# Latents' norm inside the projection, and index scores, queries and keys as one program

## The reference, cut to what matters

```python
mod = cond @ w_ada[l] + b_ada[l]
sh1, sc1, gt1, sh2, sc2, gt2 = [m[:, None, :] for m in jnp.split(mod, 6, axis=-1)]
h = rms_norm(x, g_pre_mix[l]) * (1.0 + sc1) + sh1
proj = h @ w_in[l]
(c_q, c_kv, k_rope, q_d, k_d, v_d, q_idx, k_idx, w_idx) = jnp.split(proj, split_at, axis=-1)
y_mla = mla_attention(c_q, c_kv, k_rope, positions, g_q_a[l], g_kv_a[l], w_q_b[l], w_kv_b[l])
y_dsa = dsa_attention(q_d, k_d, v_d, q_idx, k_idx, w_idx, positions)
mix = jnp.concatenate([y_mla, y_dsa], axis=-1) @ w_o[l]
x = x + gt1 * rms_norm(mix, g_post_mix[l])
h2 = rms_norm(x, g_pre_ffn[l]) * (1.0 + sc2) + sh2
ffn = moe_ffn(h2, w_router[l], b_router[l], w_mlp1[l], b_mlp1[l], w_mlp2[l], b_mlp2[l])
```

## Time and profile before

| | |
|---|---|
| Median of 3 runs | 3205.06 us (3203.02 to 3207.84) |
| The profiled execution | 3207.77 us |
| Its span in the profile | 3206.0 us, granted clock 0.919 on average |
| Busy: PE, DVE, ACT, POOL | 2899.5, 2155.3, 1628.3, 180.7 us |
| First mixer, up to the residual | about 515 us |

### The profile page before, as it was taken

One profiled execution on the slowest core, in us unless ns is written; L12 is line 12 of the kernel. 1 busy time (PEld: TensorE's weight loads), 2 busy tenths in 40 slices (PEclk: granted clock), 3 DMA queues, 4 the chain that ended last, 5 costly groups with the idle time before them and its releaser, 6 DMA issues. The chain is left out here.

```text
span 3206.0 us, 40971 instructions
## 1 busy us (share of the span) xinstructions
PE 2899.5 (90%) x13449; PEld 2295.6 (72%) x13449; DVE 2155.3 (67%) x3059; ACT 1628.3 (51%) x2117; POOL 180.7 (6%) x137
## 2 busy tenths in 40 slices
PE   7758895399999999999998698899999988899998
PEld 6636574278888888888887475578887765588887
DVE  5459635399999999999997764654444465554444
ACT  6323422378888888888886324433222324342222
POOL 2600200200000000000000300000000000000000
PEclk9865576699999999999999798999999999999999
DMA  7439512399999999999997521132332320233222
GB/s 267 144 113 353 212 54 112 132 355 386 389 391 376 390 390 386 381 391 389 381 384 294 190 69 38 53 99 92 99 99 92 112 59 27 67 105 98 93 85 92
DMA packets 292798, 660.39 MB, mean 206 GB/s; under 512 B 21850, under 2 KB 146538, under 8 KB 292676
## 3 DMA queue, kind: packets, MB, share of 16 engines
q1 hardware_dynamic: 275890, 603.45, 51.0%
q0 software_dynamic: 10816, 37.11, 3.1%
q10 hardware_dynamic: 5970, 18.21, 1.4%
HBM read 583.12 MB, written 75.58 MB: 205 GB/s over the span
## 5 line engine op out<-in xcount | busy, mean ns | idle before, releaser
L1530 DVE TENSOR_TENSOR weights_low<-pieces,weights_high 128x1024 fp32r<-128x1024 f32 x768 | 890.4, 1220 | 72.2 <-ACT weights_high L1523 63.0
L1523 ACT ACTIVATE weights_high<-pieces 128x1024 fp32r<-128x1024 f32 x768 | 804.9, 1062 | 201.3 <-PE banks L378 201.2
L376 PE MATMUL banks<-weights_high,xT_high 128*128 128x512 f32 x1024 | 403.1, 394 | 1.3 <-DVE weights_low L1530 1.3
L377 PE MATMUL banks<-weights_low,xT_high 128*128 128x512 f32 x1024 | 399.6, 390 | 0.0
L378 PE MATMUL banks<-weights_high,xT_low 128*128 128x512 f32 x1024 | 399.1, 390 | 0.0
L2145 ACT ACTIVATE weights_high<-pieces 128x1024 fp32r<-128x1024 f32 x192 | 200.8, 1053 | 322.6 <-DMA pieces<-in_w_up 248.9
L2149 DVE TENSOR_TENSOR weights_low<-pieces,weights_high 128x1024 fp32r<-128x1024 f32 x192 | 233.6, 1223 | 126.2 <-ACT weights_high L2145 124.9
L376 PE MATMUL banks<-hT_high,weights_high 128*128 128x512 f32 x704 | 284.3, 404 | 2.8 <-DVE hT_low L3171 2.8
L377 PE MATMUL banks<-hT_low,weights_high 128*128 128x512 f32 x704 | 276.3, 393 | 0.0
L378 PE MATMUL banks<-hT_high,weights_low 128*128 128x512 f32 x704 | 275.5, 391 | 0.0
L376 PEld LDWEIGHTS banks<-weights_high,xT_high 128*128 128x128 f32 x1024 | 192.8, 188 | 52.9 <-issue 13.5
(11 more groups left out here) (448 smaller groups left out, 4662.3 us busy)
## 6 DMA issues: line engine op xcount, KB each, us to landing
pieces<-in_w_mlp SPq DMA_DIRECT2D x768, 512.0 KB, 7.7
expert_out<-mask SPq DMA_DIRECT2D x32, 1536.0 KB, 15.0
pieces<-in_w_up SPq DMA_DIRECT2D x64, 512.0 KB, 3.9
pieces<-in_w_down SPq DMA_DIRECT2D x64, 512.0 KB, 3.3
pieces<-in_w_in SPq DMA_DIRECT2D x56, 512.0 KB, 4.8
pieces<-in_w_ada SPq DMA_DIRECT2D x48, 512.0 KB, 5.1
expert_out<-y ACTq DMA_DIRECT2D x32, 512.0 KB, 7.8
pieces<-in_w_out SPq DMA_DIRECT2D x16, 512.0 KB, 4.8
```

The costliest lines, as they stand in the source:

```text
L376: nc.tensor.matmul(out, a[0], b[0], start=start, stop=False)
L377: nc.tensor.matmul(out, a[0], b[1], start=False, stop=False)
L1523: self.core.nc.scalar.activation(self.hi[:, c % E_PARTS, :], self.raw[:, c % E_RAW, :], ACT.Copy).then_inc(self.high.sem, 1)
L1530: self.core.nc.vector.tensor_tensor(self.lo[:, c % E_PARTS, :], self.raw[:, c % E_RAW, :], self.hi[:, c % E_PARTS, :], ALU.subtract).then_ ...
```

## The change

The late jobs leave the projection and the opening: 20 run in the second attention (three in four units from the seventh) and 15 in the product with w_o, two behind each piece from the third on; the zero writes are now six and five there, one behind every third load. The ring places that held late pieces in the projection hold the latents' weights (`Latents`), which SP loads first in the projection. The squares, the root, the scalings and the transposes of the latents, and the rotation of the shared key, are done inside `projection_stage`, while the second and third column blocks run; it uses six banks and leaves two for the transposes. `index_stages` and the rest of `mla_stages` ahead of the attention become `middle_stage`, one block: for each tile PE makes queries, keys and values, then six index scores (two banks), then turns queries and keys (through the same two banks). ACT instead of DVE copies keys and values out. Relu buffers are four instead of two.

```diff
-LATE_FIRST, LATE_SECOND = 24, 11
+LATE_FIRST, LATE_SECOND = 20, 15
...
-def projection_stage(core, pieces, hT, xT, cols, widths, proj, late):
+def projection_stage(core, pieces, hT, xT, cols, widths, proj, latent, cos, sin, W):
...
-        @block.gpsimd
-        def _(pool):
-            late.add(pool, LATE_FIRST)
         @block.sync
         def _(sp):
+            latent.load(sp, W)
             for q in range(count * PIECES - pieces.places):
                 pieces.load_piece(sp, count * PIECES)
-            late.load(sp, LATE_FIRST)
...
-            for p in range(first + PIECES, first + count * PIECES):
+            for p in range(first + PIECES, first + 2 * PIECES):
                 pieces.split_high(act, p)
-                late.scale(act, LATE_FIRST // (2 * PIECES))
-            late.scale(act, LATE_FIRST - late.scaling)
+            for i in range(2 * T):
+                act.wait_ge(*taken(i % T + 1))
+                if i:
+                    act.wait_ge(*squares(i))
+                part = proj[:, i % T, OFF1[i // T]:OFF1[i // T + 1]]
+                nc.scalar.activation(core.junk[:, 0, 0:part.shape[1]], part, ACT.Square, accum_out=stats[:, 6 * T + i:6 * T + i + 1]).then_inc(squares.sem, 1)
+            pieces.split_high(act, first + 2 * PIECES)
+            act.wait_ge(*spread(1))
+            nc.scalar.activation(rt, ms, ACT.Sqrt).then_inc(root.sem, 1)
+            for c in range(3):
+                act.wait_ge(*lat_turned(c + 1))
+                nc.scalar.activation(latent.latT[:, c, :], core.psum[:, 6 + c % 2, :], ACT.Copy).then_inc(lat_taken.sem, 1)
+            for p in range(first + 2 * PIECES + 1, first + 3 * PIECES):
+                pieces.split_high(act, p)
...
-                    if k == 0 and i >= 8:
-                        pe.wait_ge(*taken(i - 7))
+                    if k == 0 and i >= 6:
+                        pe.wait_ge(*taken(i - 5))
...
+                    last = product_in_parts(nc, core.psum[:, i % 6, 0:width], tokens, w, k == 0, k == KD - 1)
+                    if n == 1 and k == KD - 1 and t == 2:
+                        for c in range(3):
+                            pe.wait_ge(*lat_ready(1))
+                            if c == 2:
+                                pe.wait_ge(*lat_taken(1))
+                            for s in range(T):
+                                last = nc.tensor.transpose(core.psum[:, 6 + c % 2, s * P:(s + 1) * P], proj[:, s, c * P:(c + 1) * P], core.ident[:])
+                            last.then_inc(lat_turned.sem, 1)
...
             for n in range(count):
                 for t in range(T):
                     i = n * T + t
-                    if n + 1 < count:
-                        pieces.split_low(dve, first + (n + 1) * PIECES + t)
+                    if n == 0:
+                        pieces.split_low(dve, first + PIECES + t)
+                    if n == 1 and t in (0, 3):
+                        pieces.split_low(dve, first + 2 * PIECES + t // 3)
+                    if n == 2 and t == 0:
+                        pieces.split_low(dve, first + 2 * PIECES + 2)
+                        pieces.split_low(dve, first + 2 * PIECES + 3)
                     dve.wait_ge(*(product(n * (T - 1) + t + 1) if t < T - 1 else pieces.used(first + (n + 1) * PIECES)))
-                    nc.vector.tensor_copy(proj[:, t, n * BANK:n * BANK + widths[n]], core.psum[:, i % 8, 0:widths[n]]).then_inc(taken.sem, 1)
+                    if n == 1 and t == 0:
+                        dve.wait_ge(*squares(2 * T))
...
+                    if n == 1 and t == 1:
+                        dve.wait_ge(*root(1))
+                        step(nc.vector.reciprocal(rstd, rt))
+                        dve.wait_ge(*latent.gains_full(32))
+                        for s in range(T):
+                            cq, ckv = proj[:, s, 0:Q_RANK], proj[:, s, OFF1[1]:OFF1[2]]
+                            nc.vector.scalar_tensor_tensor(out=cq, in0=cq, scalar=rstd[:, s:s + 1], in1=latent.gq, op0=ALU.mult, op1=ALU.mult)
+                            ins = nc.vector.scalar_tensor_tensor(out=ckv, in0=ckv, scalar=rstd[:, T + s:T + s + 1], in1=latent.gkv, op0=ALU.mult, op1=ALU.mult)
+                        ins.then_inc(lat_ready.sem, 1)
+                    if n == 2 and t == 0:
+                        for s in range(T):
+                            rotate(nc, step, latent.krot[:, s], proj[:, s, OFF1[2]:OFF1[3]].unsqueeze(1), cos[:, s, :], sin[:, s, :], latent.tmp, 1, ROPE // 2)
...
         with nc.Block() as block:
             @block.sync
             def _(sp):
-                pieces.load_ahead(sp, count * PIECES)
+                for i in range(LATE_SECOND):
+                    late.load(sp, 1)
+                    if i % 3 == 2:
+                        aside(sp, range(E - LATE_SECOND // 3 + i // 3, E - LATE_SECOND // 3 + i // 3 + 1))
+            @block.gpsimd
+            def _(pool):
+                late.add(pool, LATE_SECOND)
             @block.scalar
             def _(act):
                 for p in range(first, first + count * PIECES):
                     pieces.split_high(act, p)
+                    if p >= first + 2:
+                        late.scale(act, 2)
+                late.scale(act, LATE_SECOND)
...
-                    late.add(pool, LATE_SECOND)
+                    late.add(pool, LATE_FIRST)
...
-                    if late is not None and u >= H1 and u % 2:
-                        late.scale(act, 1)
+                    if late is not None and u >= 6 and u % 4 != 3:
+                        late.scale(act, min(1, LATE_FIRST - late.scaling))
...
                 pieces.load_ahead(sp, count * PIECES)
-                late.load(sp, late.places)
...
+    def __init__(self, core, ring):
+        flat = ring.rearrange("p a n -> p (a n)")
+        self.latT = flat[:, 0:3 * S].rearrange("p (c n) -> p c n", c=3)
+        self.wq = flat[:, 3 * S:3 * S + 2 * H1 * QK1].rearrange("p (c n) -> p c n", c=2)
+        self.wkv = flat[:, 3 * S + 2 * H1 * QK1:3 * S + 2 * H1 * QK1 + H1 * (NOPE + VDIM)]
+        spare = core.junk[:, 0, :]
+        self.tmp = spare[:, 256:256 + 4 * (ROPE // 2)].rearrange("p (a h n) -> p a h n", a=4, h=1)
+        self.gq, self.gkv = spare[:, 512:512 + Q_RANK], spare[:, 768:768 + KV_RANK]
+        self.krot = spare[:, 896:896 + T * ROPE].rearrange("p (t h n) -> p t h n", t=T, h=1)
...
+            def _(pe):
+                def turn_index():
+                    for c in range(2):
+                        for t in range(T):
+                            last = nc.tensor.transpose(core.psum[:, 4 + c, t * P:(t + 1) * P], proj[:, t, qio + c * P:qio + (c + 1) * P], core.ident[:])
+                        last.then_inc(idx_turned.sem, 1)
...
+                def make(t):
+                    tile = slice(t * P, (t + 1) * P)
+                    if t:
+                        pe.wait_ge(*rotated(t))
+                        pe.wait_ge(*k_rows(t))
+                    w = 4 * QK1
+                    for n in range(2):
+                        for c in range(2):
+                            last = nc.tensor.matmul(core.psum[:, n, 0:w], latT[:, c, tile], wq[:, c, n * w:(n + 1) * w], start=(c == 0), stop=(c == 1))
+                    last.then_inc(q_made.sem, 1)
+                    for n in range(2):
+                        last = nc.tensor.matmul(core.psum[:, 2 + n, :], latT[:, 2, tile], wkv[:, n * BANK:(n + 1) * BANK], start=True, stop=True)
+                    last.then_inc(kv_made.sem, 1)
+                def scores(i):
+                    t, h = tiles[i]
+                    if i >= 2:
+                        pe.wait_ge(*relu(i - 1))
+                    g = (h % 4) * IDX_D
+                    nc.tensor.matmul(core.psum[:, 6 + i % 2, 0:(t + 1) * P], qiT[g:g + IDX_D, h // 4, t * P:(t + 1) * P], kiT[g:g + IDX_D, 0:(t + 1) * P], start=True, stop=True).then_inc(score.sem, 1)
+                def turn(src, j):
+                    if j:
+                        pe.wait_ge(*taken(2 * j))
+                    for h in range(H1):
+                        last = nc.tensor.transpose(core.psum[0:QK1, 4 + h // 4, (h % 4) * P:(h % 4 + 1) * P], src[:, h, :], core.ident[:])
+                    last.then_inc(turned.sem, 1)
+                turn_index()
+                pe.wait_ge(*latent.weights_full(32))
+                make(0)
+                pe.wait_ge(*idx_taken_a(2))
+                pe.wait_ge(*idx_taken_d(1))
+                for t in range(T):
+                    if t:
+                        make(t)
+                    for i in range(6 * t, 6 * t + 6):
+                        scores(i)
+                    pe.wait_ge(*rotated(t + 1))
+                    turn(qk, 2 * t)
+                    pe.wait_ge(*k_rows(t + 1))
+                    pe.wait_ge(*k_rope(t + 1))
+                    turn(kk, 2 * t + 1)
+                def take_index(j, dst, bank):
+                    act.wait_ge(*idx_turned(j))
```

(110 more changed lines are left out.)

208 lines of the change are left out of this document (44 added, 164 removed).

## The result

The kernel after took 3173.05 us in the median (3168.78 to 3177.7), the kernel before beside it 3204.95 (3203.02 to 3207.84): a ratio of 0.990 (95% interval 0.9883 to 0.9917), 31.9 us faster. The forecast was 3170.3 with a range of 3153 to 3191. The profiled execution has a span of 3175.6 us against 3206.0, 30.4 less.

A forecast was written before the change was run, and what follows sets the result against it. Each stage had its own limit: the projection PE's waits behind late jobs, the first attention DVE, the second PE. Terms -15.7 - 24.6 + 1.5 + 4 = -34.8 took 3205.1 to 3170.3 us, range 3153 to 3191.

The forecast's parts named there:

- Term 1: Projection: late jobs leave it and the latents' norm hides under the product, only its transposes on the path; minus 15.7 us.
- Rival F: Projection: scaled latents ready many us behind PE's third tile, so it only trades its waits; total 3186 us, chance 4%.
- Term 2: Middle: one block of 61 us instead of 85.6, at a granted clock of 0.8; minus 24.6 us.
- Rival D: Middle: runs at full clock in 52 us; total 3161.3 us, chance 13%.
- Term 3: Second attention: nine more late scales on ACT and adds on POOL cost time in the first tiles; plus 1.5 us.
- Term 4: Product with w_o: ACT's late scales wait for loads and delay weight splits that PE needs; plus 4 us.
- B: Middle: runs at half clock in 84 us; total 3193.3 us, chance 10%.
- C: Late jobs hold PE again in their new places and all 15.7 us come back; total 3180.5 us, chance 15%.
- E: Second attention and product: each group of late loads and a zero write takes 17.4 us; total 3232 us, chance 3%.

The follow-up runs named there:

- the filled kernel: Kernel after with one added TensorE product per middle tile, placed in the wait before the keys are turned: middle 54.8 us, total 3162.52 us (one execution).
- both edits together: Kernel after with keys turned into banks 2 and 3 and the product's first four late loads issued in the second attention: 3155.59 us, ratio 0.9851 to before.
- the early transfers alone: Kernel after with the first four late loads of the product issued at the end of SyncE's list in the second attention: 3167.64 us, ratio 0.9893 to before.
- the kernel with the keys' banks: Kernel after with keys turned into banks 2 and 3, so PE does not wait for ACT's query copies: 3157.64 us, ratio 0.9852, middle 47.5 us.

## Why the prediction held, and where it did not

**Term 1, right.** -15.3 against -15.7: the last matmul ended at about 122.5 where 123.5 was forecast (the opening's 1.4 us are in that), the latents were ready 1.7 us ahead of PE's question for them, the margin of the forecast, both 1.5 us earlier, and the transposes cost the 1.9 us that I had put on the path (46.2 against 44.3 without the norm). The split of 1.22 us in the earlier trace rows, read as one alone, had an addition of POOL beside it (from 62.05, 5.41 us); the value held all the same, as the second block's pieces were split in 1.22 us with POOL gone. Rival F, that the projection trades its waits, is out.

**Term 2, right in its parts, off by the clock.** The waits are those that I named. I took a granted clock of 0.8 from the tiles of the earlier trace rows; it was 0.74. The formula of the forecast, 52 + 32 x (1/clock - 1) + 1, gives 64.2 us for 0.74, and 63.6 were measured; for 0.96 it gives 54.3, less the 5.0 of waits 49.3, and 47.5 were measured. The failed step is to take the clock as given. It moved with the pauses that the new order leaves. The earlier trace rows could have warned: transposes at half clock stood close behind the idle time of the rotation. I read this as a price of transposes, but the first eight of the earlier trace rows ran at full, 1.08 us, as did those of the keys in the filled kernel, 1.04. Nor does one pause set the pace of the next group: that 1.08 stands right behind 3.20 us of idle time.

Rival D, full clock in the middle, nearly came true once the pause of 1.26 us per tile was gone or filled: 0.96 and 0.91, at 47.5 and 54.8 us. The Trainium skill, "TensorE: Matmul & The Clock Gate", Part 1, describes a kernel in which short idle moments between groups of matmuls make the clock swing between its levels; the pair with and without filled waits agrees (0.91 against 0.74). The Trainium skill's rule in the same part, that sustained work brings the full clock, is again not borne out by the second attention, where PE was busy 88.6 of 88.6 us at 0.50.

**Term 3, right by number, wrong by reason.** +1.6 against +1.5, but the late jobs cost nothing: without them the stage took 113.5. What went is a part of the stretch at full clock near its start (0.67 against 0.85 over 9.8 us). The step that nine more scalings and additions push PE in the first tiles failed: PE's own time covers them. That the number fitted is luck. Why the identical set-up is granted the full clock for longer in some executions is open: both kernels with the old middle had it (111.9), and one in nine with the new. With PE kept busy ahead of it the stage took 111.3.

**Term 4, right by mechanism, a little small.** +5.1 against +4. The stall at the fourth piece was put at 1 to 3 us and measured 2.5, that at the last piece at 2 and measured 1.1: 3.5 us together. Of the rest 0.8 us go with the clock: PE was granted 0.79 from 4 to 20 us where it had 0.89 in the kernel with only the late jobs moved, which had the same two stalls and +4.3. The stall is not the cause of that: both edits together had 0.79 without it, and took 0.9 us more than the early transfers alone at 0.89. The other 0.7 us no run names. POOL's last addition ended at 458.1, ahead of the last copy at 459.8, as forecast.

**Outside the terms.** The opening gave 1.4 us: the stretch up to the projection's first copy was granted 0.99 and not 0.93, with PE busy all through both. This can't be put down to the late jobs' leaving: the kernel with the keys' banks runs the same code up to there and took 78.1 us, at 0.93. The kernel before, then after:

```profile
58.00:78.40 20.40, 20.40 (x85) 16.69 (x84) 7.21 (x13) 12.66 (x14) 15.96 (x6) 0.93 0.44 140
...
58.00:77.00 19.00, 19.00 (x84) 15.71 (x83) 6.78 (x11) 5.69 (x6) 0.00 (x0) 0.99 0.39 141
```

The sum: -1.4 - 15.3 - 22.5 + 1.6 + 5.1 + 2.0 = -30.5, of 30.4 in the spans. Rivals B, C and E are out: the middle's clock was 0.74 and not half, and the late jobs held PE for 5.1 us and not 15.7. ACT did wait for late pieces in the product, 13.2 us in six waits, but the 15 loads with their five zero writes were through by 458.1, where E had 87 us for the stage.

## What to carry to other kernels

- Cost a short recurring wait of TensorE twice: once for itself, and once for the clock of the work about it. Here 1.26 us four times were worth 5 us of waiting and about 11 by the clock; give the second result banks of its own before anything else is reordered.
- Work moved beside a full engine needs its data there: place its first transfers one stage ahead of its first use, or the wait lands in the queue of an engine that others need. Here that took 3.7 of 5.1 us off the stage; the rest stayed.
- A matching total doesn't prove a term. Leave the supposed cause out and look whether the time goes with it.

## What was unexpected of the hardware

- Adding four products to the middle made it 8.8 us shorter (63.6 to 54.8 us), as the granted clock rose from 0.74 to 0.91. Each added product took 1.0 to 1.9 us.
- Same instructions, other clock: the kernel after's middle took 61.2, 63.6, 63.7 and 65.1 us in four executions, and unchanged code behind the mixer 2705 to 2716. For such a stage a difference under 4 us between two single profiles is weak evidence.
- With 20 additions of GpSimd (47.7 us busy) beside the second attention VectorE was busy 54.1 us of 88.6, and 42.4 without them, and the stage took 113.6 and 113.5: TensorE had no idle time in either.
